# A two-layer diffusion backbone on one core: every large matrix product in one plain fp32 multiplication

## The reference, cut to what matters

```python
def run_layer(x, cvec, l, attend):
    mod = ada_modulation(cvec, w_ada[l], b_ada[l])          # (silu(c) @ w_ada + b), six vectors
    h = rms_norm(x, norm_g[l, 0]) * (1 + sc_m) + sh_m
    y, k, v = token_mixer(h, w_in[l], w_out[l], ...)         # h @ w_in -> attention, gMLP, conv -> @ w_out
    x = x + gt_m * rms_norm(y, norm_g[l, 1])
    h = rms_norm(x, norm_g[l, 2]) * (1 + sc_f) + sh_f
    if l % 2 == 0: f = swiglu(h, w_ffn_gu[0], w_ffn_d[0])    # (silu(g) * u) @ w_d, D_FF = 2816
    else:          f = moe_swiglu(h, w_router[0], w_moe_gu[0], w_moe_d[0])  # top 2 of 8 experts
    x = x + gt_f * rms_norm(f, norm_g[l, 3])
```

## Time and profile before

| | us |
|---|---|
| median of three executions | 1781.12 (1780.52 to 1782.64) |
| the profiled execution | 1779.33 |
| its span | 1777.6 |
| TensorE busy | 1650.7 (93% of the span) |
| VectorE busy | 1089.5 |
| ScalarE busy | 926.5 |
| stage: start to the first product of layer 0 | 0 to 47 |
| layer 0, input and output projection | 47 to 263 |
| dense layer and its residual | 263 to 573 |
| layer 1, input projection up to the router | 573 to 826.6 |
| six experts of one tile each | 826.6 to 1412.8 |
| two experts of one tile and a half | 1412.8 to 1743 |
| sum, norm, output | 1743 to 1777.6 |

### The profile page before, as it was taken

One profiled execution on the slowest core, in us unless ns is written; L12 is line 12 of the kernel. 1 busy time (PEld: TensorE's weight loads), 2 busy tenths in 40 slices (PEclk: granted clock), 3 DMA queues, 4 the chain that ended last, 5 costly groups with the idle time before them and its releaser, 6 DMA issues.

```text
span 1777.6 us, 21764 instructions
## 1 busy us (share of the span) xinstructions
PE 1650.7 (93%) x8658; PEld 1293.1 (73%) x8658; DVE 1089.5 (61%) x1204; ACT 926.5 (52%) x1137; POOL 170.9 (10%) x178
## 2 busy tenths in 40 slices
PE   5799979999998899975999999999999999999993
PEld 2567758888776567754887877878787777787782
DVE  2336563333235326644998989898988866657653
ACT  1425452323225325453777777777777755455541
POOL 2400000000003000002021020303030100010001
PEclk9999979999998999986999999999999999999996
DMA  9973223333465872315999999999999976676643
GB/s 334 342 263 143 90 72 110 127 119 119 166 234 153 294 261 84 99 63 169 358 369 350 378 350 376 349 381 350 370 358 358 357 217 209 213 228 211 202 155 120
DMA packets 295809, 422.11 MB, mean 237 GB/s; under 512 B 21792, under 2 KB 226592, under 8 KB 295584
## 3 DMA queue, kind: packets, MB, share of 16 engines
q1 hardware_dynamic: 281504, 394.85, 65.7%
q0 software_dynamic: 13056, 23.11, 4.3%
q10 hardware_dynamic: 1136, 2.64, 0.4%
HBM read 418.56 MB, written 19.27 MB: 246 GB/s over the span
## 4 chain that ended last, share of the span: by engine, by line
PE 85%; DMA 4%; DVE 4%; ACT 2%; issue 2%; SPq 1%; POOL 1%; POOLq 0%; DVEq 0%; ACTq 0%
PE ps L1287 23%; PE ps L1289 22%; PE ps L1288 22%; PE ps L1293 3%; PE ps L1294 3%; DMA raw<-in_w_in_dram 2%; PE ps L1643 2%; PE ps L1329 1%; PE ps L1721 1%; SPq L436 1%; PE ps L1354 1%; DMA raw<-in_w_ada_dram 1%; PE ps L1477 1%; PE ps L1461 1%; PE ps L1311 1%
## 5 line engine op out<-in xcount | busy, mean ns | idle before, releaser
L890 DVE TENSOR_TENSOR wlo<-raw,whi 128x2048 fp32r<-128x2048 f32 x327 | 747.3, 2291 | 327.4 <-ACT whi L628 324.7
L628 ACT ACTIVATE whi<-raw 128x2048 fp32r<-128x2048 f32 x327 | 625.9, 1917 | 341.4 <-DMA raw<-in_w_in_dram 108.7
L1287 PE MATMUL ps<-whi,xhi 128*128 128x512 f32 (+1 forms) x1352 | 546.3, 404 | 18.2 <-DVE wlo L890 11.0
L1289 PE MATMUL ps<-whi,xlo 128*128 128x512 f32 (+1 forms) x1352 | 528.3, 391 | 0.0
L1288 PE MATMUL ps<-wlo,xhi 128*128 128x512 f32 (+1 forms) x1352 | 527.7, 390 | 0.0
L1287 PEld LDWEIGHTS ps<-whi,xhi 128*128 128x128 f32 x1352 | 258.2, 191 | 86.8 <-DVE wlo L890 25.2
L1289 PEld LDWEIGHTS ps<-whi,xlo 128*128 128x128 f32 x1352 | 257.6, 191 | 54.2
L1288 PEld LDWEIGHTS ps<-wlo,xhi 128*128 128x128 f32 x1352 | 258.5, 191 | 47.7 <-issue 0.5
L1287 PE MATMUL ps<-whi,hhi 128*128 128x512 f32 x484 | 196.3, 405 | 0.4 <-DVE pg L1007 0.4
L1289 PE MATMUL ps<-whi,hlo 128*128 128x512 f32 x484 | 189.5, 391 | 0.0
L1288 PE MATMUL ps<-wlo,hhi 128*128 128x512 f32 x484 | 189.1, 391 | 0.0
(11 more groups left out here) (219 smaller groups left out, 1287.8 us busy)
## 6 DMA issues: line engine op xcount, KB each, us to landing
raw<-in_w_moe_gu_dram SPq DMA_DIRECT2D x352, 512.0 KB, 6.5
raw<-in_w_moe_d_dram SPq DMA_DIRECT2D x176, 512.0 KB, 6.3
raw<-in_w_ada_dram SPq DMA_DIRECT2D x96, 512.0 KB, 10.0
raw<-in_w_in_dram SPq DMA_DIRECT2D x44, 512.0 KB, 7.5
raw<-in_w_ffn_gu_dram SPq DMA_DIRECT2D x44, 512.0 KB, 4.6
raw<-in_w_ffn_d_dram SPq DMA_DIRECT2D x22, 512.0 KB, 6.9
raw<-in_w_out_dram SPq DMA_DIRECT2D x16, 512.0 KB, 4.4
bias<-rpb_rows POOLq DMA_DIRECT2D x32, 96.0 KB, 4.3
```

The costliest lines, as they stand in the source:

```text
L628: act.activation(whi[m % SPL][:, :], raw[n % RING][:, :], ACT.Copy).then_inc(s_hi, 1)
L890: dve.tensor_tensor(wlo[n % RING][:, :], raw[n % RING][:, :], whi[NTH[n] % SPL][:, :].bitcast(F32), ALU.subtract).then_inc(s_lo, 1)
L1287: pe.matmul(out, a_hi, w_hi, start=start, stop=False)
L1289: return pe.matmul(out, a_lo, w_hi, start=False, stop=stop)
```

## The change

Every large product becomes one `pe.matmul` of fp32 operands, read from the ring and from one copy of the activations. `whi`, `wlo`, `xlo`, `hlo` and all `split` work are gone, `xT` and `hT` take the place of the copies, and the work of writing them is shared: even blocks by ACT, odd blocks by DVE. TensorE waits for a chunk's transfer itself. The class of 129 to 192 tokens is dropped, so such an expert runs as two tiles. The ring has ten slots.

```diff
-SHAPES = [(1, 0), (1, 1), (2, 0), (3, 0)]
-RING = 6
+RING = 10
-SPL = 3
...
-        wlo = [nc.alloc_sbuf_tensor_at(f"wlo{i}", [P, CHUNK], F32R, offset=ring + 4 * CHUNK * i) for i in range(RING)]
-        whi = [sb(f"whi{i}", [P, CHUNK], F32R) for i in range(SPL)]
-        xhi = sb("xhi", [P, KT, NT * P], F32R)
-        xlo = sb("xlo", [P, KT, NT * P], F32R)
+        xT = sb("xT", [P, KT, NT * P])
...
-        hhi = at("hhi", 0, [P, FK, NT * P], F32R)
-        hlo = at("hlo", 33792, [P, FK, NT * P], F32R)
+        hT = at("hT", 0, [P, FK, NT * P])
...
+        def arrived(eng, n):
+
+            eng.wait_ge(s_raw[n % RING], 32 * (n // RING + 1))
+
+        def x_ready(eng, s, kt):
+
+            eng.wait_ge(s_xtd if kt % 2 else s_xta, KT // 2 * s + kt // 2 + 1)
...
@@ scalar, norm
-                upto(n_next)
                 act.wait_ge(s_modc, 2 * l + half + 1)
-                for kt in range(KT):
+                for kt in range(0, KT, 2):
...
-                    ins = act.activation(hf[:, kt, P:3 * P], p6[:, P:3 * P], ACT.Identity,
+                    ins = act.activation(xT[:, kt, P:3 * P], p6[:, P:3 * P], ACT.Identity,
...
@@ scalar, gate_up
-                    upto(n0 + 2 * b + 3)
                     act.wait_ge(s_pe, n0 + 2 * b + 2)
...
-                        hi(b - 1)
+                        turned_h(b - 1)
...
@@ vector, norm
-                for kt in range(KT if s < 3 else 0):
-                    dve.wait_ge(s_hf, KT * s + kt + 1)
-                    dve.tensor_copy(xhi[:, kt, :], hf[:, kt, :]).then_inc(s_xhi, 1)
-                    dve.wait_ge(s_xhi, KT * s + kt + 1)
-                    dve.tensor_tensor(xlo[:, kt, :], hf[:, kt, :], xhi[:, kt, :].bitcast(F32), ALU.subtract
-                                      ).then_inc(s_xlo, 1)
+                for kt in range(1, KT, 2):
+                    dve.wait_ge(s_tr, KT * s + kt + 1)
+                    sh, sc = modc[:, 2 * half, kt, :], modc[:, 2 * half + 1, kt, :]
+                    for g, a, b in ((0, 0, P), (1, P, 3 * P)):
+                        ins = dve.tensor_scalar(xT[:, kt, a:b], ps[:, banks[kt], a:b], sc[:, g:g + 1], sh[:, g:g + 1],
+                                                ALU.mult, ALU.add)
+                    ins.then_inc(s_xtd, 1)
...
@@ vector, the gathered rows
-                dve.wait_ge(s_ghi, KT * e + kt + 1)
-                dve.tensor_tensor(xlo[:, kt, :], ps[:, 6 + kt % 2, 0:NT * P], xhi[:, kt, :].bitcast(F32),
-                                  ALU.subtract).then_inc(s_glo, 1)
+                dve.wait_ge(s_ga, KT * e + kt + 1)
+                dve.tensor_copy(xT[:, kt, :], ps[:, 6 + kt % 2, 0:NT * P]).then_inc(s_gxd, 1)
...
@@ tensor, win
-                    pe.wait_ge(s_lo, NTH[n] + 1)
-                    hi, lo = halves(n, kk)
+                    arrived(pe, n)
+                    w = chunk(n, kk)
...
-                            ins = three(ps[:, t, 0:width], xhi[:, kt, a:a + P], xlo[:, kt, a:a + P],
-                                        hi[:, i, :], lo[:, i, :], kt == 0, last)
+                            ins = pe.matmul(ps[:, t, 0:width], xT[:, kt, a:a + P], w[:, i, :],
+                                            start=(kt == 0), stop=last)
...
@@ tensor, gate_up
-                                ins = three(ps[:, 2 * t + b % 2, :], xhi[:, kt, P * t:P * t + P],
-                                            xlo[:, kt, P * t:P * t + P], hi[:, kk, :], lo[:, kk, :],
-                                            kt == 0, kt == KT - 1)
-                        if half:
-                            if b == 0 and h == 0:
-                                free(1)
-                                pe.wait_ge(s_pack, k)
-                            for kk in range(4):
-                                kt = 4 * h + kk
-                                ins = two(ps[:, 2 + b % 2, :], xhi[:, kt, P:2 * P], hi[:, kk, :], lo[:, kk, :],
-                                          kt == 0, kt == KT - 1)
+                                ins = pe.matmul(ps[:, 2 * t + b % 2, :], xT[:, kt, P * t:P * t + P], w[:, kk, :],
+                                                start=(kt == 0), stop=(kt == KT - 1))
```

More of the change, by code:

```diff
@@ L418, in by_tiles @@
             leave(1, 0)
-            for kind, (tiles, half) in zip(kinds, SHAPES):
+            for kind in kinds:
                 for e in range(NE):
                     nc.switch_bb(label(kind, e), parent=entry)
-                    part(tiles, half, e)
+                    part(kind, e)
                     leave(kind, e + 1)
@@ L696, in _, with gate_up, turned_h @@
             act.activation(sil[:, :, :], sil[:, :, :], ACT.Silu).then_inc(s_sil, 1)
[L698 to L706, removed]
+            def gate_up(T, k, n0):
+                def turned_h(b):
+                    act.wait_ge(s_ht, k * 2 * GU_B + 2 * b + 1)
+                    act.activation(hT[:, 2 * b, 0:P * T], ps[:, 6, 0:P * T], ACT.Copy).then_inc(s_hta, 1)
                 for b in range(GU_B):
-                    upto(n0 + 2 * b + 3)
                     act.wait_ge(s_pe, n0 + 2 * b + 2)
@@ L1283, in pe_done, with chunk @@
                 ins.then_inc(s_pe, 1)
-            def three(out, a_hi, a_lo, w_hi, w_lo, start, stop):
-                pe.matmul(out, a_hi, w_hi, start=start, stop=False)
-                pe.matmul(out, a_hi, w_lo, start=False, stop=False)
-                return pe.matmul(out, a_lo, w_hi, start=False, stop=stop)
-            def two(out, a, w_hi, w_lo, start, stop):
-                pe.matmul(out, a, w_hi, start=start, stop=False)
-                return pe.matmul(out, a, w_lo, start=False, stop=stop)
-            def halves(n, k):
-                return (whi[NTH[n] % SPL][:, :].rearrange("p (k n) -> p k n", k=k),
-                        wlo[n % RING][:, :].rearrange("p (k n) -> p k n", k=k))
+            def chunk(n, k):
+                return raw[n % RING][:, :].rearrange("p (k n) -> p k n", k=k)
             def ada_turn(l, i):
@@ L1557, in win, with down @@
                         mix(l)
-            def down(T, hi_of, lo_of, place, nk, wait, s_done, between=None, even_banks=None, bank=lambda t: 2 * t,
-                     half=0, first=None, before=None):
+            def down(T, aT, place, nk, wait, s_done, between=None, even_banks=None, bank=lambda t: 2 * t,
+                     first=None, before=None):
                 for q in range(nk // 2):
                     wait(q)
-                    hi, lo = halves(place(q), 2)
-                    steps = [(t, h) for h in (1, 0) for t in range(T + half)] if q == 0 else [
-                        (t, h) for t in range(T + half) for h in (1, 0)]
+                    w = chunk(place(q), 2)
+                    steps = [(t, h) for h in (1, 0) for t in range(T)] if q == 0 else [
+                        (t, h) for t in range(T) for h in (1, 0)]
                     if q == 0 and first is not None:
@@ L1612, in between @@
                     if q == 2:
-                        pe.wait_ge(s_mlo, KT * (l + 1))
+                        mix_ready(pe, l, KT - 2)
+                        mix_ready(pe, l, KT - 1)
                         gates(2 * l, gate_m)
                 steps = [(2, 1), (0, 0), (0, 1), (1, 0), (1, 1), (2, 0)]
-                down(NT, xhi, xlo, lambda q: PLACE["wout", l, q], KT, wait, s_y, between, first=steps, before=before)
+                down(NT, xT, lambda q: PLACE["wout", l, q], KT, wait, s_y, between, first=steps, before=before)
             def gates(s, gate):
@@ L1654, in gate_up @@
                     for h in range(2):
-                        pe.wait_ge(s_lo, NTH[n0 + 2 * b + h] + 1)
-                        hi, lo = halves(n0 + 2 * b + h, 4)
+                        arrived(pe, n0 + 2 * b + h)
+                        w = chunk(n0 + 2 * b + h, 4)
                         for t in range(T):
@@ L1694, in even_banks @@
                     pe.wait_ge(s_pm, (k + 1) * GU_B)
-                down(T, hhi, hlo, place, FK, wait, s_done, then, even_banks if T + half > 1 else None, bank, half)
+                down(T, hT, place, FK, wait, s_done, then, even_banks if T > 1 else None, bank)
             def dense():
```

301 lines of the change are left out of this document (98 added, 203 removed).

## The result

The changed kernel takes 2125.16 us, median of four executions (2123.51 to 2125.54), where the kernel before took 1781.88 in the same comparison: a ratio of 1.1923, with a 95% interval of 1.1902 to 1.1944. The prediction was 2175 us, range 2143 to 2210. The direction and the largest term, the price of a product, were right; the term of what comes back was less than half of what it measured, and the time lies 18 us under the range.

The account below looks back on a forecast made before the run. The prediction took TensorE as the bound, busy 1650.7 of 1777.6 us. Adding 429.5 us for products and taking off 35 coming back gave a 2172.1 us span, 2175 us as measured time, range 2143 to 2210.

Parts of the forecast that it names:

- the price of a product: On TensorE, each full product goes from 0.680 to 0.858 us, half-tile ones from 0.453; all product terms together +429.5 us.
- what comes back: Idle and cold time regained in layers, norms, experts and the end: 35 us together, between none and 60.
- loads in the open: Rival: in dense rows each record pays 0.429 + 0.19 us because its load is not hidden; 2955 us, chance 0.03.
- four passes at 0.227: Rival: each plain fp32 product makes four passes at the old pace; 2278 us, chance 0.05.
- The faster rival: Two records per product at the rounded pace, 0.454 us a product, one-tile experts gaining nothing; 1520 us, chance 0.03.
- There it waits for nobody: In the experts TensorE is always busy, so a dearer product lengthens the span by just that much.
- nearly level: In the six one-tile experts, transfers at 359 GB/s with a share of 1.05 are almost as full as TensorE.
- Priced at nothing: Transposes in the last two experts: same number, 44 wider ones costing TensorE tenths of a microsecond in all.
- The layers: Both layers, start and router: 31 us back, from idle time, cold clock and the norms.
- the step over `xhi` and `xlo`: At the norms, the way from normalised block to first product gets shorter: 4.7 us in two places, 5 in all.
- The ring: Ten slots fill during the residual before layer 1's input projection, where 9 of 10.9 us come back.
- The upper bound on what returns, 60: All idle and cold time of the named stretches with the rest: at most 60 us back.

Follow-up runs that it names:

- e2_noclass: The kernel before, rounded products kept, without the class of 129 to 192 tokens: 1825.89 us.
- e1_two: The kernel before with the experts' chunks left unsplit and two rounded multiplications instead of three in each expert product: 1714.69 us.
- e5_form: The kernel before with only its products exchanged for one plain fp32 multiplication each, splits and waits kept: 2168.98 us, ratio 1.218.
- table of four runs: The kernel before with and without the experts' splits: six one-tile experts 586.4 and 578.9 us under full transfers, 575.7 and 574.6 with a quarter of the bytes.
- e3_wide: The kernel before with the half tile transposed whole, 128x128 in place of 64x64: 1772.89 us, ratio 0.9942.
- e7_form_wide: e5_form with the half tile transposed whole: 2157.31 us in one execution.

## Why the prediction was right, and where it failed

The price of the longer product, 429.5 us in the sum, held. What failed is the term beside it, what comes back: 83.4 us in place of 35, and over the 60 that I gave as its upper bound.

- **The bound and the price of a product: right.** TensorE was full and stayed so; a product is two records of 0.429 us. The changed kernel's last two experts take 92.8 us more than e2_noclass's, which has the same 528 products in the rounded form: 0.176 each, where I had 0.178. The 2052 products and both rivals with a dearer product (loads in the open, four passes at 0.227) are settled by the loads above. The Trainium skill says "4 passes" for true fp32 (FP8 and Floating Point Precision, TensorE Precision Notes). The 0.858 us of a product agree with it if a pass takes 0.215 us, an estimate (0.858 / 4), two passes to a record; no run here shows the passes themselves. It was my reading at the rounded form's 0.227 that gave too much.
- **The faster rival: its place was real, its price wasn't.** e1_two ran at that price in the experts, and the six one-tile experts gained 16 us of a possible 180, as the rival's own working said: the transfers hold them.
- **"There it waits for nobody": the step that failed first.** I read 586.18 busy of 586.20 us as no waiting, and gave nothing back in the six experts beside the transfers at a share of 1.05 which I called "nearly level". It gave back 17.0. 14.5 came with the longer product alone (e5_form), 2.5 with a clock that had risen before the stage. The table of four runs shows transfers and splits together costing 10.8 of the rounded form's time, at full clock, and the loads waited for DVE's remainder 39 times. So the earlier trace rows, a list of the matmuls' waits alone, was no price for the splits.
- **"Priced at nothing": the transposes of the half, mis-sized by 8 to 12 us** (e3_wide, e7_form_wide). I had them cost tenths of a microsecond in all. With the pack and the handling of the half the last two experts gave back 18.0 in place of 3; 4.3 of it came with the longer product alone.
- **The layers: 46.8 in place of 31.** The parts I named (waits for splits, the clock they cost, the step over `xhi` and `xlo`) are there: no wait for a split is left, and layer 1's projection came back with 168.4 + 23.5 - 175.3 = 16.6 us, where I had 14. But I took a part of each idle time and nothing for `wout` and the norms' surroundings. About half, 23.9, came with the longer product alone, and TensorE's idle time fell by 14.2 us of it (table of the layers). Which small delays make up that half stays open; waits for attention's DVE steps and for `f` in the norms are 6 us of it (4.8 to 2.2, and 21.4 to 17.8 in the lists of waits).
- **The ring: a wrong reason beside a fair size.** I gave 9 us in layer 1 partly to the ten slots; six do as well.
- **The upper bound on what returns, 60, was no bound.** It was put as the sum of idle and cold time, but the terms given add up to about 45: 36.0 in the four stretches of the layers and 9 for norms, experts and end. And whatever the sum, the delays under a record's modelled end are not in it.

## What to carry to other kernels

A longer instruction on a full engine costs its count times its difference, less everything that had been just late under it; where transfers or helpers are level with that engine, run the stage's instructions at another pace (or the transfers at a quarter) before calling the returned part zero. Where ends are modelled, read fullness from the distances between starts and from the waits of the weight loads, not from busy time. And plain fp32 products of 512 columns at 0.858 us cost more here than three rounded ones at 0.68, although all the splitting work went; a kernel in which the splitting engines end last was not run.

## What the runs showed of the hardware that I had not expected

- A 64x64 transpose between whole ones made every change cost 0.20 us or more, where whole ones follow each other after 0.11: the smaller instruction was the dearer one.
- Plain fp32 records kept their 0.429 us across changes of chunk and under 0.91 of DMA share: over the six experts of the changed kernel the mean is 0.4294, with one distance out of 1469 above 0.441. The rounded records had a mean of 0.2287 even without the late ones, and 0.2280 with a quarter of the transfers and no splits.
